# Pairing the key and value steps of the sample group between projection tiles of a two-layer decoder trunk

## What is computed

```python
h = rms_norm(x, g_mix[l]); proj = h @ w_in[l]
rq, rk, rv, rg, mq, mk, mv, gate_r, gate_a = split_proj(proj)
rq, rk = retnet_rotate(rq, pos), retnet_rotate(rk, pos) * R_DK ** -0.5      # retention
# samples' attention, per sequence and head: keep 3 of 4 past blocks of 256 keys
means = mean(k_pages over block); idx = top_k(q . means, 3)
p = softmax([q . k_selected, q . k_own] * M_DH ** -0.5); mo = p @ [v_selected, v_own]
merged = sigmoid(gate_r) * (ro @ w_br_ret[l]) + sigmoid(gate_a) * (mo @ w_br_att[l])
x = x + merged @ w_out[l]   # then RMSNorm, SwiGLU FFN, residual
```

## Time and profile before

| | |
|---|---|
| median of 3 runs | 1921.45 us (1921.27 to 1921.62) |
| the profiled execution | 1918.65 us, its span 1916.9 us |
| PE busy | 1893.9 us, 99% of the span |
| DVE busy | 1333.4 us, 70% |
| ACT busy | 814.3 us, 42% |
| POOL busy | 201.7 us, 11% |
| mean granted clock | 0.998 |

### The profile page before, as it was taken

One profiled execution on the slowest core, in us unless ns is written; L12 is line 12 of the kernel. 1 busy time (PEld: TensorE's weight loads), 2 busy tenths in 40 slices (PEclk: granted clock), 3 DMA queues, 4 the chain that ended last, 5 costly groups with the idle time before them and its releaser, 6 DMA issues. The chain is left out here.

```text
span 1916.9 us, 39547 instructions
## 1 busy us (share of the span) xinstructions
PE 1893.9 (99%) x16267; PEld 1778.8 (93%) x16267; DVE 1333.4 (70%) x1902; ACT 814.3 (42%) x1287; POOL 201.7 (11%) x289
## 2 busy tenths in 40 slices
PE   8999999999999999999999999999999999999998
PEld 8968879999999999999998797899899999999998
DVE  6686544367765888988676775444686568889876
ACT  4372323333434464655433633223243344555453
POOL 2250120012000011212000002101110000000000
PEclk9999999999999999999999999999999999999999
DMA  7768781255244346666444288423543442433332
GB/s 256 270 221 298 268 277 56 89 174 170 89 157 135 89 145 178 168 177 172 134 155 163 89 292 296 161 78 111 179 155 111 126 133 80 133 110 89 110 95 86
DMA packets 275108, 300.60 MB, mean 157 GB/s; under 512 B 14538, under 2 KB 225650, under 8 KB 274418
## 3 DMA queue, kind: packets, MB, share of 16 engines
q1 hardware_dynamic: 249778, 208.53, 34.5%
q0 software_dynamic: 25024, 89.41, 14.4%
q10 hardware_dynamic: 128, 0.15, 0.0%
HBM read 273.00 MB, written 58.59 MB: 173 GB/s over the span
## 5 line engine op out<-in xcount | busy, mean ns | idle before, releaser
L2036 DVE TENSOR_TENSOR WL<-RAW,WH 128x2048 fp32r<-128x2048 f32 (+2 forms) x76 | 161.1, 2120 | 79.9 <-ACT WH L1485 79.8
L925 PE MATMUL PS<-XH,WH 128*128 128x272 f32 x960 | 203.3, 293 | 0.6
L925 PE MATMUL PS<-XL,WH 128*128 128x272 f32 x960 | 198.3, 288 | 0.0
L925 PE MATMUL PS<-XH,WL 128*128 128x272 f32 x960 | 197.8, 287 | 0.0
L1485 ACT ACTIVATE WH<-RAW 128x2048 fp32r<-128x2048 f32 (+2 forms) x84 | 149.8, 1784 | 25.1 <-PE PS L925 18.8
L1391 PE MATMUL PS<-KQ,CH 128*128 128x272 f32 x1088 | 158.3, 288 | 1.5 <-DVE KQ L2622 1.5
L925 PEld LDWEIGHTS PS<-XH,WH 128*128 128x128 f32 x960 | 150.4, 188 | 7.8 <-issue 5.2
L905 PE MATMUL PS<-WH,XH 128*128 128x256 f32 x512 | 150.8, 294 | 0.5 <-ACT EA L1507 0.5
L925 PEld LDWEIGHTS PS<-XL,WH 128*128 128x128 f32 x960 | 150.9, 188 | 0.0
L925 PEld LDWEIGHTS PS<-XH,WL 128*128 128x128 f32 x960 | 150.3, 189 | 0.0
L1391 PEld LDWEIGHTS PS<-KQ,CH 128*128 128x128 f32 x1088 | 145.0, 188 | 2.2 <-issue 2.2
(11 more groups left out here) (464 smaller groups left out, 5105.2 us busy)
## 6 DMA issues: line engine op xcount, KB each, us to landing
RAW<-in_w_in SPq DMA_DIRECT2D x94, 512.0 KB, 5.9
keys_laid<-in_cache_k POOLq DMA_DIRECT2D x128, 256.0 KB, 3.7
RAW<-in_w_gu SPq DMA_DIRECT2D x128, 256.0 KB, 4.2
PG<-keys_laid SPq DMA_DIRECT2D x16, 1024.0 KB, 8.5
RAW<-in_w_down SPq DMA_DIRECT2D x64, 256.0 KB, 4.2
RAW<-in_w_gu SPq DMA_DIRECT2D x24, 512.0 KB, 5.1
PG<-in_cache_v POOLq DMA_DIRECT2D x40, 256.0 KB, 4.5
PG<-in_cache_v SPq DMA_DIRECT2D x40, 256.0 KB, 4.3
```

The source lines that it names most:

```text
L925: last = pe.matmul(PS[:, 2 * pair + h, 0:HALF], w[:, i, c0:c0 + P], block[:, h * HALF:(h + 1) * HALF], start=first and i == 0 and a == 0, ...
L2036: dve.tensor_tensor(WL[:, slot, 0:n], RAW[:, slot, 0:n], WH[:, slot, 0:n].bitcast(F32), ALU.subtract).then_inc(lo_ready, 1)
```

## The change

Two tables take the place of the even spread. The steps of each period come in pairs: K4 K5, K6 K7, ... K14 K15, and V0 V1, V2 V3, ... V14 V15. All tiles that belong to a pair stand ahead of its first step. Nothing else is edited: the buffers, the loads and their conditions, the places of `split_at`, `select`, `exp_group` and the turns stay as they are.

```diff
+    VALUE_ROWS = {3: (0, 1), 4: (1, 4), 6: (4, 6), 8: (6, 10), 10: (10, 13), 12: (13, 16), 14: (16, 19)}
+    LATE_ROWS = {2: (5, 8), 4: (8, 9), 6: (9, 10), 8: (10, 13), 10: (13, 15), 12: (15, 18), 14: (18, 20)}
+
     def value_rows(q):
 
-        n = V_STEP - FIRST_STEPS
-        return range((q - FIRST_STEPS) * (4 * TT - 1) // n, (q + 1 - FIRST_STEPS) * (4 * TT - 1) // n) if q >= FIRST_STEPS else ()
-
-    VALUE_STEPS = (2, 3, 5, 6, 7, 8, 10, 11, 12, 13, 14, 15)
+        return range(*VALUE_ROWS.get(q, (0, 0)))
 
     def late_rows(i):
 
-        if i not in VALUE_STEPS:
-            return []
-        n = VALUE_STEPS.index(i)
-        return [TT + n // 4 * TT] * (n % 4 == 0) + [TT + n // 4 * TT + 1 + n % 4]
+        return range(*LATE_ROWS.get(i, (0, 0)))
```

## The result

| | before | after |
|---|---|---|
| median | 1921.45 us (1919.67 to 1921.62, 5 runs) | 1933.81 us (1929.04 to 1939.55, 5 runs) |
| the profiled execution | 1918.65 us, span 1916.9 us | 1935.25 us, span 1933.6 us |
| mean granted clock of the runs | 0.998 in the profiled one | 0.990 to 0.995, 0.994 in the profiled one |
| ratio to before | | 1.0070, 95% interval [1.0059, 1.0081] |

The change makes the kernel 12.4 us slower. The forecast was 6.7 us slower, 1928.1 us, with a range up to 1932.0: the direction is right, the size is not, and the time lies outside the range. Lines of the changed kernel stand three lower than in the rows of before; those of e1 to e3 stand two lower.

What follows compares the result with a forecast made beforehand. PE, busy for 99% of the span, was taken as the bound, so new waits count in full. Gains of 6.6 and 2.1 us against the losses summed to +6.7 us on the median of 1921.45: 1928.1 us, range 1916 to 1932.

Steps and rivals of the forecast that it cites:

- passages: Going out of the fp32r token tiles to a run of steps and back: 20 fewer at 0.33 us, 6.6 us gained.
- K4's waits: PE's waits at K4 for DVE's turn of its page, 1.24 and 0.87 us, would go: 2.1 us gained.
- new wait 1: At K7, whose page turn follows the later split at q = 4 on DVE: 0.6 us lost for both layers.
- new wait 2: Tile behind S at V0 V1: late split at q = 14 delays select(1) and the bank, 3.0 us each layer, 6.0 lost.
- group 0: Same pattern with select(0) behind the split at q = 7 and two turns: 0.2 us each layer, 0.4 lost.
- new wait 3: At V7, whose pages can be sent only after V4 and land late: 2.8 us each layer, 5.6 us lost.
- V15: Its last page lands too late behind V12: 0.65 us short, 1.3 us lost in all, bound 0 to 2.
- clock: Granted clock falling to 0.50 behind new idle stretches on PE: one fall, 1.5 us lost, 0 to 6 in all.
- A: Rival: pages and copies come in time at V7 and the tile behind S, passages won; 1915.2 us, faster; chance 0.16.
- B: Rival: one of the two large waits is small, for example V7's, and no clock falls; 1922.5 us; chance 0.26.
- C: Rival: pairing also makes key pages K8 and K9 late, with a further clock fall; 1932.9 us, slower; chance 0.13.
- The page rule: Skill's estimate of 2.6 us for a 256 KB transfer; by it V7 would be 0.3 us late in each layer.

Runs made afterwards that it cites:

- e1: Key period in the changed kernel's order, value period in the order of the kernel before: 1921.64 us, ratio 1.0008 to the kernel before.
- e3: Value period in the changed kernel's order, key period in the order of the kernel before: 1933.11 us, ratio 1.0075 to the kernel before.
- e8: Against the kernel before: keys in pairs, split at q = 12, only V10 V11 and V14 V15 paired among values: 1915.0 us, ratio 0.9972.
- e5: The changed kernel with the fourth weight split moved from q = 14 to q = 12: 1930.91 us, ratio 1.0054 to the kernel before.
- e9: The changed kernel unedited, run once more: 1940.96 us, ratio 1.0085 to the kernel before.
- e2: Paired keys and old value order, with the fourth weight split moved from q = 14 to q = 12: 1916.88 us, ratio 0.9980 to the kernel before.
- e6: The changed kernel with two token tiles moved, from ahead of V2 and V4 to ahead of V4 and V6: 1919.37 us, ratio 0.9994.

## Why the prediction was right and where it failed

| term | forecast, us | measured in the profiled execution of after, us |
|---|---|---|
| passages, 20 | -6.6 | -6.6 (by the 0.33 each of e8) |
| K4's waits | -2.1 | -2.1, both gone |
| new wait 1, K7 | +0.6 | +0.6 (0.28 each) |
| new wait 2, third `rqb` tile | +6.0 | +5.8 (2.90 and 2.92) |
| group 0 | +0.4 | none seen |
| new wait 3, V7 | +5.6 | +5.1 (2.87 and 2.25) |
| V15 | +1.3 | +2.6 (1.65 and 0.98) |
| sum without the clock | +5.2 | +5.4 |
| clock | +1.5 | +7.3 (1.5, 1.6, 2.7 and 1.5, 17.0 us at half clock) |
| K0 and K3, before any edited place | 0 | +3.5 |
| sum | +6.7 | +16.2, of 16.6 between the two profiles |

The four parts of the clock's term are read from starts. The third `rqb` tile to V2 takes 4.55 and 4.52 us, and 3.01 at full clock in e5; V7 to V9 is worked out above; 2.7 came behind V15 of layer 0. The other 0.4 us are not assigned. The medians lie 12.4 us apart and not 16.6, because the profiled execution of before lies 2.8 us below its median and that of after 1.4 above.

**What held.** That PE is the bound, which two arrivals become late, and in which order of events each does. The idle and the passages together were forecast at +5.2 and came to +5.4. The execution of e9 whose clock stayed at 0.997 took 1928.18 us, and with PE kept busy in the waits the median was 1925.5, 4.9 us above the kernel before beside it (1920.57). Rivals A and B (a large wait small or gone) and C (key pages late) did not happen: K8 and all key steps behind it run on time.

**The step that failed** is the one headed "The clock": "I take one fall, 1.5 us lost". It had the price of a fall from one place, K3, and counted one fall of 3.4 us for four idle stretches that it had itself put at 2.3 to 3 us, in the size of K3's. The count should have followed the prediction's own comparison ("nearest to the first"). With four falls at its own 1.7 us the forecast would have been 1933.4. In the traces here all nine idle stretches of 2.69 us or more in these periods brought the clock down, K3's left out, and three of the seven between 1.6 and 2.4 us did; K3's, of 2.63 to 5.13 us, did in all eleven profiles. The length was the second fault: half clock lasted 3.4 us at K3 in the profile of before, but 6.8 at K3 in those of e2 and e9, and 3.4, 6.8 or 10.2 behind the new waits. What sets the length is not shown. The 1.7 us for 3.4 at half clock was nearly right (1.5 to 1.6). With four falls of 3.4 to 6.8 us at 0.46 the term would have been 6 to 12.5 us and the forecast about 1933 to 1939, which holds the median. The count of four is right in part by luck: one of the four large waits had none behind it, and V15 of layer 0, at 1.65 us, had one.

**The range** ended at 1932.0, although the clock's own bound of 6 us in the text gives 1928.1 + 4.5 = 1932.6 alone. A bound that was written down was not carried through to the range.

**V15** was the term mis-sized among the waits: 0.65 us each forecast, 1.65 and 0.98 measured. In layer 0 the page left on time and landed after 6.5 us where the earlier trace rows have 5.5; in layer 1 it took 5.5, but left 4.12 us behind V12 instead of 3.78. V7's landed after 5.2 and 4.6 us, where the earlier trace rows have 4.8 and 5.5: later in layer 0, earlier in layer 1, 0.5 us less for both. Such landings spread by about 1 us, and the 2.6 us for both layers are outside the bound of 0 to 2.

**K0 and K3 of layer 0.** The prediction said that K3 and its wait stay as they are. In the profile of before K3 waits 2.9 us, in those of e2, e3 and e6 2.6 to 2.8, in all others 4.2 to 5.1, whether the keys are paired or not, and no step or tile ahead of it was moved in any of them. What makes its page land at one time or the other stays open. It stands in the difference of the two profiled executions (3.5 us), and since it comes and goes from profile to profile whatever the edit, it is not counted as a cost of the change; it must be taken out before the two profiles are set against each other.

**The page rule** behind rival B. The last page of V7 landed 5.2 and 4.6 us after its issue and V15's after 6.5 and 5.5 us. By the Trainium skill's page "SBUF — State Buffer", section "The DMA setup-cost knee", 256 KB would take an estimated 2.6 us. The traces disagree by a factor of about two, as they did before the change. Here pages for two steps leave close together; that this is the reason is not shown, since no run sends one alone.

## What to carry to other kernels

Packing small work of one kind together saves a passage each time (0.33 us here), but it shortens the time that a buffer has between its last use and its next. Before pairing, add up for each buffer the issue and the landing of its refill and compare it with the work on PE that is left in between, and leave out the pairs that come up short. e8 does this, moves the late split as well, and wins 5.2 us where the full pairing loses 12.4. And on an engine that is the bound, price idle stretches like these at one and a half to two times their length: here 13.6 us of new idle brought 17.0 us at half clock behind it in one execution and 30.6 in another, by the prices above an estimated 7 and 13 us of time, and with it a spread from run to run that the idle itself does not have.

## What the runs showed of the hardware that was not expected

**The same waits give different clocks.** One kernel, two profiled executions: 17.0 and 30.6 us at half clock behind the same waits, and medians of two sets of runs of 1933.81 and 1940.96 us, with single executions from 1928.18 to 1941.9. The time follows the mean granted clock: 1928.18 at 0.997, 1929.04 at 0.995, 1932.98 and 1933.81 at 0.993, 1939.55 and 1941.9 at 0.990. Of all nine executions the middle one is 1935.25. The Trainium skill's page "TensorE: Matmul & The Clock Gate", section "What's actually happening", calls the slow stretch at a kernel's start variable from run to run; here the same shows in the middle of a kernel. Its section "Terms" puts the penalty at half of the time at half clock; the rows give 0.46 of what lies behind the wait, so the trace nearly agrees.

**Short idle can bring the clock down too, not each time.** The clock fell behind 1.65 us of idle at V15 in layer 0 of the changed kernel, behind 1.93 us in layer 0 of e1 and not behind the same 1.93 us in layer 1, not behind 1.92 us at V15 in e9, and behind 1.13 us at V15 in layer 1 of e5, the only one of thirteen idle stretches between 0.9 and 1.4 us.

**What a wait is worth depends on the waits beside it.** In e5 4.6 us of idle were taken out at one tile and 2.9 us of time won, and its profile has longer falls behind the waits that were left; in e6 it was 7.7 us of idle and 14.4 us of time, and no fall was left. The gain of e5 lies within the spread of the changed kernel's own executions (1928 to 1942 us), so its size is not shown; that of e6 is clear of it.
